# One stage in place of two: output projection, norm and FFN of a layer

## The reference, cut to what matters

```
x = x + gate1 * (mixed @ w_out)                 # output projection, 1024 x 1024
h = rmsnorm(x, norm2_g) * (1 + scale2) + shift2 # mean of squares over the 1024 features of a token
a, b = split(h @ w_ffn_in)                      # 1024 x 5632
x = x + gate2 * ((silu(a) * b) @ w_ffn_out)     # 2816 x 1024
```

## Time and profile before

| | |
|---|---|
| median of 3 runs | 3119.05 us (3117.54 to 3120.02) |
| the profiled execution | 3119.82 us, of which the span is 3118.0 us |
| TensorE busy | 2794.0 us, 90% of the span |
| VectorE busy | 1394.4 us, 45% |
| ScalarE busy | 832.1 us, 27% |
| GpSimd busy | 727.8 us, 23% |
| mean granted TensorE clock | 0.947 |

### The profile page before, as it was taken

The page is one execution under the profiler, slowest core; times in us unless marked ns, Lnnn a source line. Parts: engine busy times, 40 slices in busy tenths (PEclk is TensorE's granted clock), DMA queues, the critical chain, the costliest instruction groups (busy, mean ns, idle before and its releaser), DMA issues. The chain is left out here.

```text
span 3118.0 us, 41354 instructions
## 1 busy us (share of the span) xinstructions
PE 2794.0 (90%) x16562; PEld 2658.8 (85%) x16562; DVE 1394.4 (45%) x2937; ACT 832.1 (27%) x1235; POOL 727.8 (23%) x279
## 2 busy tenths in 40 slices
PE   6994886969999999999589996889699999999995
PEld 4994775969999999999479995549699999999994
DVE  6996885672322222223445554543623222222235
ACT  4112665052111111111442222541521111111114
POOL 1551123142112211111231112332421122111110
PEclk9996998979999999999799997999899999999997
DMA  5433100412111111110223335304021111111101
GB/s 229 144 120 78 21 8 33 173 58 81 41 40 40 40 50 44 40 40 0 114 77 142 142 123 203 105 19 176 34 81 41 40 40 41 51 43 40 40 0 61
DMA packets 59395, 225.92 MB, mean 72 GB/s; under 512 B 7136, under 2 KB 20128, under 8 KB 49696
## 3 DMA queue, kind: packets, MB, share of 16 engines
q1 hardware_dynamic: 57712, 224.07, 20.3%
q10 hardware_dynamic: 1584, 0.51, 0.1%
HBM read 190.47 MB, written 29.88 MB: 71 GB/s over the span
## 5 line engine op out<-in xcount | busy, mean ns | idle before, releaser
L420 PE MATMUL ps<-hh,wi_hi 128*128 128x384 f32 x2112 | 710.3, 336 | 8.9 <-POOL hl L335 4.6
L421 PE MATMUL ps<-hl,wi_hi 128*128 128x384 f32 x2112 | 709.5, 336 | 0.0
L422 PE MATMUL ps<-hh,wi_lo 128*128 128x384 f32 x2112 | 709.4, 336 | 0.0
L802 DVE TENSOR_TENSOR hid<-ps,hid 128x384 f32<-128x384 f32 x132 | 73.4, 558 | 1048.6 <-ACT hid L712 1019.3
L420 PEld LDWEIGHTS ps<-hh,wi_hi 128*128 128x128 f32 x2112 | 399.0, 189 | 12.8 <-POOL hl L335 5.6
L421 PEld LDWEIGHTS ps<-hl,wi_hi 128*128 128x128 f32 x2112 | 399.4, 189 | 0.0
L422 PEld LDWEIGHTS ps<-hh,wi_lo 128*128 128x128 f32 x2112 | 399.2, 189 | 0.0
L712 ACT ACTIVATE hid<-ps 128x384 f32<-128x384 f32 x132 | 65.0, 493 | 1178.1 <-PE ps L422 1178.1
L792 DVE SCALAR_TENSOR_TENSOR x<-ps,mod,x 128x128 f32<-128x128 f32 (+1 forms) x704 | 327.3, 513 | 77.7 <-PE ps L422 72.9
L735 POOL TENSOR_TENSOR wi_lo<-raw_in,wi_hi 128x2048 fp32r<-128x2048 f32 x44 | 202.5, 4604 | 681.4 <-ACT wi_hi L703 681.4
L421 PE MATMUL ps<-hid_lo,wo_hi 128*128 128x384 f32 x1056 | 353.0, 334 | 0.0
(11 more groups left out here) (231 smaller groups left out, 3983.2 us busy)
## 6 DMA issues: line engine op xcount, KB each, us to landing
raw_in<-in_w_ffn_in_dram SPq DMA_DIRECT2D x44, 1024.0 KB, 4.7
wmt<-in_w_mod_t_dram SPq DMA_DIRECT2D x80, 512.0 KB, 3.6
raw_out<-in_w_ffn_out_dram SPq DMA_DIRECT2D x22, 1024.0 KB, 4.7
gla_spill<-turn SPq DMA_DIRECT2D x24, 576.0 KB, 2.8
raw<-in_w_in_odd_dram SPq DMA_DIRECT2D x24, 512.0 KB, 3.9
wm<-in_w_mod_dram SPq DMA_DIRECT2D x16, 512.0 KB, 11.3
raw<-in_w_in_even_dram SPq DMA_DIRECT2D x16, 512.0 KB, 4.4
x<-in_x_dram SPq DMA_DIRECT2D x4, 1152.0 KB, 9.6
```

What stands on the lines that cost most here:

```text
L420: pe.matmul(acc, w_hi, in_hi, start=first, stop=False)
L421: pe.matmul(acc, w_hi, in_lo, start=False, stop=False)
L422: return pe.matmul(acc, w_lo, in_hi, start=False, stop=last)
L802: dve.tensor_tensor(hid[:, t], ps[:, 2 * t + 1, 0:CW], hid[:, t], ALU.mult).then_inc(hid_done, 1)
```

## The change

`projection` and `ffn` of a layer become one stage, `trunk`, with one instruction order written out by hand for each engine:

- x is loaded in four transfers of two tiles each (`stream`) straight into x and is updated in place. `x_old` is gone. SyncE issues only the first of the four ahead of weight tiles 2 and 3.
- `whi` and `wlo` have three buffers each. Tiles 0 to 5 are multiplied as before. The last pair is multiplied third by third: (6,0), (7,0), (6,1), (7,1), (6,2), (7,2).
- Squares are taken on ScalarE as each third of each tile is finished, and summed on GpSimd (`Seam.square`, `Seam.total`), into the space of `raw_out`.
- The norm is done for each third on its own: mean by TensorE, Ln and Exp by ScalarE, `scale` by VectorE, shift and high part together by ScalarE, low part by VectorE. It is placed among the last tiles of the projection and the first blocks of pass 0.
- In pass 0 the six hidden blocks run one after the other, and the contractions of thirds 0 and 1 follow.
- The first FFN weights are loaded, cast and split during tiles 4 to 6.
- In `ModulationBeside`, one instruction over 1024 columns takes the place of four over 256 with their final sum. This holds for all four stages that use it. In `trunk` each third of a tile has one modulation tile beside it, from third 0 of tile 0 on, until the 16 (layer 0) or 8 (layer 1) are used up.

The diff, cut to its core (`Attended` and `Ready`, which did nothing, go; semaphores and buffer offsets are left out):

```diff
-                for g in range(self.SEGS):
-                    seg = slice(g * w, (g + 1) * w)
-                    last = dve.scalar_tensor_tensor(out=self.unused[:, 0, seg], in0=self.wmt[t % 2][:, seg], scalar=1.0,
-                                                    in1=self.silu_row[:, v, seg], op0=ALU.mult, op1=ALU.mult,
-                                                    accum_out=self.part[:, t, v, g:g + 1])
...
+                if 2 * n + v:
+                    dve.wait_ge(self.wmt_used, 2 * n + v)
+                dve.scalar_tensor_tensor(out=self.unused, in0=self.wmt[n % 2][:], scalar=1.0, in1=self.silu_row[:, v],
+                                         op0=ALU.mult, op1=ALU.mult, accum_out=self.acc[:, n % 4, v:v + 1]).then_inc(self.wmt_used, 1)
...
+        def total(self, pool, ft, c):
+            e, a = self.place[ft, c]
+            if a is None:
+                return
+            pool.wait_ge(self.squared, e + 1)
+            if a:
+                pool.wait_ge(self.summed, a)
+            pool.tensor_tensor(self.stat[:, c], self.stat[:, c], self.sq[a % 2][:], ALU.add).then_inc(self.summed, 1)
+        def mean(self, pe, c, bank):
+            pe.wait_ge(self.summed, self.adds[c])
+            pe.matmul(bank, ones[:], self.stat[:, c], start=True, stop=True).then_inc(self.averaged, 1)
+        def root(self, act, c, bank):
+            act.wait_ge(self.averaged, c + 1)
+            act.activation(self.stat[:, c], bank, ACT.Ln, bias=eps[:], scale=1.0 / D).then_inc(self.logged, 1)
+            act.wait_ge(self.logged, c + 1)
+            act.activation(self.stat[:, c], self.stat[:, c], ACT.Exp, scale=-0.5).then_inc(self.rooted, 1)
+        def scale(self, dve, c, kk):
+            if kk == 0:
+                dve.wait_ge(self.rooted, c + 1)
+            for cols, v in pieces[c]:
+                loc = slice(cols.start - c * CW, cols.stop - c * CW)
+                last = dve.scalar_tensor_tensor(out=hl_f32[:, kk, cols], in0=x[:, kk, cols], scalar=amod[:, self.n, kk, v:v + 1],
+                                                in1=self.stat[:, c, loc], op0=ALU.mult, op1=ALU.mult)
+            last.then_inc(self.scaled, 1)
+        def high_part(self, act, c, kk):
+            act.wait_ge(self.scaled, KT * c + kk + 1)
+            for cols, v in pieces[c]:
+                last = act.activation(hh[:, kk, cols], hl_f32[:, kk, cols], ACT.Identity,
+                                      bias=mod[:, self.layer, self.shift * KT + kk, v:v + 1])
+            last.then_inc(self.high, 1)
+        def low_part(self, dve, c, kk):
+            dve.wait_ge(self.high, KT * c + kk + 1)
+            for cols, v in pieces[c]:
+                last = dve.scalar_tensor_tensor(out=hl[:, kk, cols], in0=hl_f32[:, kk, cols],
+                                                scalar=mod[:, self.layer, self.shift * KT + kk, v:v + 1],
+                                                in1=hh[:, kk, cols].bitcast(F32), op0=ALU.add, op1=ALU.subtract)
+            last.then_inc(self.low, 1)
+        def through(self, dve, c, a, b):
+            for kk in range(a, b):
+                if kk < KT:
+                    self.scale(dve, c, kk)
+                if kk >= 2:
+                    self.low_part(dve, c, kk - 2)
...
+    def trunk(layer, w_dram, residual, in_hi, in_lo, first_mod, groups, scales=()):
...
+            tile_off = [o, o + 2 * WB, W0 + 12 * WB]
...
+            bank_at = lambda m, c: ps[:, NC * (m % 2) + c, 0:CW]
+            mean_bank = [ps[:, b, 0:CW] for b in (0, 3, 5)]
...
+                def stream(g):
+                    sp.dma_start(x[:, 2 * g:2 * g + 2], residual[:, 2 * g:2 * g + 2]).then_inc(x_in[g], 16)
...
+                weights(0)
+                weights(1)
+                stream(0)
+                mods.load_row(sp)
+                mods.load(sp, 0)
+                mods.load(sp, 1)
+                weights(2)
+                weights(3)
+                for g in range(1, KT // 2):
+                    stream(g)
+                for n in range(2, MODS):
+                    mods.load(sp, n)
+                    if n % 3 == 1 and n // 3 + 3 < KT:
+                        weights(n // 3 + 3)
+                for m in range(min((MODS - 1 - 1) // 3 + 3, KT - 1) + 1, KT):
+                    weights(m)
+                load_in(0, 0)
+                load_in(0, 1)
+                sp.wait_ge(norm.scaled, KT * NC)
+                load_out(0)
...
+                cast(0)
+                cast(1)
+                mods.silu(act)
+                cast(2)
+                for m in range(LAST - 1):
+                    for c in range(NC):
+                        square(m, c)
                 cast_in(0, 0)
                 cast_in(0, 1)
-                norm.act_late(act)
-                body(0, first=True)
+                for c in range(NC):
+                    square(LAST - 1, c)
+                square(LAST, 0)
+                square(LAST + 1, 0)
+                square(LAST, 1)
+                norm.root(act, 0, mean_bank[0])
+                for kk in range(KT):
+                    norm.high_part(act, 0, kk)
+                    if kk == KT // 2:
+                        square(LAST + 1, 1)
+                square(LAST, 2)
+                square(LAST + 1, 2)
+                norm.root(act, 1, mean_bank[1])
+                for kk in range(KT):
+                    norm.high_part(act, 1, kk)
+                silu(0, 0, 0)
+                norm.root(act, 2, mean_bank[2])
+                for kk in range(KT):
+                    norm.high_part(act, 2, kk)
+                    if kk == KT // 2:
+                        silu(0, 0, 1)
+                hidden_high(0, 0)
+                cast_out(0)
+                silu(0, 1, 0)
...
+                pool.wait_ge(w_low, KT)
+                split_in(0, 0)
+                for c in range(NC):
+                    norm.total(pool, LAST - 1, c)
+                pool.wait_ge(multiplied, NC * LAST)
+                split_in(0, 1)
+                for c in range(NC):
+                    norm.total(pool, LAST, c)
+                    norm.total(pool, LAST + 1, c)
+                split_out(0)
...
+                tile(LAST, 0)
+                tile(LAST + 1, 0)
+                tile(LAST, 1)
+                pe.wait_ge(taken, place[LAST, 0] + 1)
+                norm.mean(pe, 0, mean_bank[0])
+                tile(LAST + 1, 1)
+                tile(LAST, 2)
+                tile(LAST + 1, 2)
+                pe.wait_ge(taken, place[LAST + 1, 0] + 1)
+                norm.mean(pe, 1, mean_bank[1])
+                pe.wait_ge(win_low, 2)
+                pe.wait_ge(norm.logged, 1)
+                pe.wait_ge(taken, place[LAST, 1] + 1)
+                hidden(0, 0, 0, first=True)
+                pe.wait_ge(taken, place[LAST + 1, 2] + 1)
+                norm.mean(pe, 2, mean_bank[2])
+                pe.wait_ge(norm.logged, 2)
+                pe.wait_ge(taken, place[LAST, 2] + 1)
+                hidden(0, 0, 1)
+                for c in (1, 2):
+                    for t in range(2):
+                        pe.wait_ge(hid_done, 2 * c + t - 1)
+                        hidden(0, c, t, first=t == 0)
+                contract(0, 0)
+                contract(0, 1)
...
+                        last = dve.scalar_tensor_tensor(out=x[:, m, cols], in0=bank_at(m, c)[:, loc],
+                                                        scalar=mod[:, layer, GATE1 * KT + m, v:v + 1], in1=x[:, m, cols],
+                                                        op0=ALU.mult, op1=ALU.add)
+                    last.then_inc(taken, 1)
...
+                for m in range(LAST):
+                    for c in range(NC):
+                        evict(m, c)
+                        if place[m, c] < MODS:
+                            mods.multiply(dve, place[m, c])
+                mods.finish(dve)
+                evict(LAST, 0)
+                evict(LAST + 1, 0)
+                evict(LAST, 1)
+                norm.through(dve, 0, 0, 5)
+                evict(LAST + 1, 1)
+                norm.through(dve, 0, 5, KT + 2)
+                evict(LAST, 2)
+                evict(LAST + 1, 2)
+                norm.through(dve, 1, 0, KT + 2)
+                gated(0, 0, 0)
+                norm.through(dve, 2, 0, 6)
+                gated(0, 0, 1)
+                norm.through(dve, 2, 6, KT + 2)
+                hidden_low(0, 0)
+                for c in (1, 2):
+                    gated(0, c, 0)
+                    gated(0, c, 1)
+                    hidden_low(0, c)
+                add(0, 0)
+                add(0, 1)
...
-    projection(inp["w_out_even"], KT, W0, residual=(inp["x"], 0, GATE1),
-               prepare=partial(Attended), mods=(6 * KT, 4, (2,)))
-    ffn(0, norm=dict(n=1, layer=0, shift=SHIFT2))
+    trunk(0, inp["w_out_even"], inp["x"], lambda kk, cols: (o_hi[kk] if kk < HEADS else p_hi[kk - HEADS])[:, cols],
```

(41 more changed lines are left out.)

508 lines of the change are left out of this document (157 added, 351 removed).

## The result

The changed kernel takes 3042.85 us (median of 4 runs, 3040.77 to 3044.89) where the kernel before takes 3118.3 (median of 4, 3117.54 to 3120.02): a ratio of 0.9763, interval 0.9751 to 0.9775. The forecast was 3041, by the case called A. The medians differ by 75.5 us, 2.4 less than the 77.8 of the forecast. The profiled execution took 3040.77 us, 79.05 less than the one before. This is where they went; a stretch's loss is its length less 0.1733 us for each product started in it, as in the prediction.

The account below looks back on a forecast made before the run. TensorE, busy 90% of the span, bounds the kernel, so only its lost stretches count: 4.1 + 8.7 + (38.7 - 5.3) + (36.9 - 5.3) = 77.8 us off 3119.8, 3042.0, median 3041; range 3032 to 3060.

Parts of the forecast that it names:

- the case called A: The forecast itself for the whole kernel, 3041 us, own range 3037 to 3047; chance 0.58.
- if TensorE waits before the first hidden block: Sign of a wrong prediction, in the seam: TensorE's first hidden block was to start at 26.6 us with no wait.
- Modulation at the end of `opening`: One 1024-column instruction, 1.28 us, lets VectorE finish sooner at the end of `opening`: 4.1 us gained, bounds 2.5 and 4.1.
- Elsewhere VectorE works beside a dense TensorE, and the saving is worth nothing: Outside the end of `opening`, the shorter modulation was to gain 0 us.
- rival E: Slower than before: VectorE becomes the projection's pace, its evictions and modulation holding up TensorE; 3143 us, chance 0.03.
- A third costs VectorE 3.5 us against 4.16, so it catches up: Projection thirds with a modulation tile: eviction 0.6 us plus multiplication 2.85, within TensorE's 4.16 us.
- Start of `trunk(0)`: Layer 0's first projection: weight tiles 2 and 3 issued earlier end the stall at tile 2; 8.7 us gained, bounds 0 and 8.8.
- The seam: Projection to FFN in each layer: 5.3 us lost, 2.4 for means and 2.9 of waits, where 38.7 and 36.9 were.
- waits at (1,1) and (2,0): In the seam, TensorE waits for gating ahead of these FFN blocks, 1.5 and 1.4 us.
- The table loads: ScalarE's norm roots: Ln and Exp each load a table, 1.28 us, by the rows; one shared set would give 3038 us.
- rival D: Means and waits in the seams all but vanish, 1.4 us to a seam; 3033 us, chance 0.07.
- Rival B: The seam's chain stretches as GpSimd stops VectorE's scalings and low parts, 8 us more a seam; 3057 us, chance 0.20.

Follow-up runs that it names:

- e2: The changed kernel with modulation's four instructions of 256 columns and their sum put back; 3064.89 us, ratio 0.9825.
- e3: The changed kernel with the old SyncE order, all of x and four modulation tiles ahead of weight tiles 2 and 3; 3051.42 us.
- e6: The changed kernel with GpSimd's sums of (6,0) and (7,0) ahead of `split_in(0,1)` and the sum of (7,1) on VectorE; 3035.76 us.
- e11: e6 with the root's Exp replaced by Identity with bias 1, so the norm is wrong, to price table loads; 3031.68 us.
- e4: The changed kernel with the sums of (6,0) and (7,0) ahead of `split_in(0,1)` on GpSimd; 3044.31 us, ratio 0.9757.
- e9: e6 with VectorE's sum of (7,1) one operation pair earlier, ahead of scaling 6; 3041.72 us, ratio 0.9755.
- e10: e9 with the last two evictions among third 0's VectorE operations, their squares earlier on ScalarE, sums of (6,2) and (7,2) on VectorE; 3035.43 us.

## Why the prediction was right, point by point

The time was right, the stall and the chain of thirds were right, and the waits of the seams were not. The prediction's own sign of being wrong, "if TensorE waits before the first hidden block", came about in both layers: mean 1 stands directly ahead of that block and waits 1.25 and 4.00 us.

- **Modulation at the end of `opening`: right.** 1.23 us for 1024 columns (1.28 forecast), first transfer at 251.21 (250.9), 3.7 us of 4.1.
- **"Elsewhere VectorE works beside a dense TensorE, and the saving is worth nothing": wrong.** With the quarters put back the changed kernel loses 13.9 us in layer 0. The step read the cost of quarters (3.0 us a tile) and the new sums on GpSimd each by itself. Together they make a third 4.45 us on VectorE, over TensorE's 4.16. The same edit that was priced at 4 us is also what keeps rival E away.
- **"A third costs VectorE 3.5 us against 4.16, so it catches up": near, and too kind.** It is 3.62, since the sum stops the second multiplication for 0.6 us each time (1.86 in place of 1.22), and with the split and the closing additions 12.5 us for a tile of 12.5. VectorE didn't catch up: it stayed 4.3 us behind until tile 5, and the FFN weights that wait for it on SyncE were late with it, and so, behind their split, was mean 0 of layer 0, while layer 1, with 8 modulation tiles, has no wait there. The argument against E, 5.3 us of GpSimd on 10.5 of VectorE, is 15.8 us for a tile of 12.5: it rules out the loss of the whole gain, not a lag of 3 us a tile, and `e2` has that lag.
- **Start of `trunk(0)`: right** in size and cause (`e3`). VectorE stood for modulation tile 2, as forecast, for 5.22 us, until 20.1 us after the first product (24 reckoned).
- **The seam: the chain was right, the waits were not.** 8.2 and 7.7 us where 5.3 was forecast. The term that failed is "Mean 0 runs 12.5 to 13.3, no wait" and "Total (7,1) is done at 23.5": the first left out that GpSimd's queue has `split_in(0,1)` ahead of the sums, the second let a sum of 1 us be 1 us beside VectorE's dense run (it was 5.49). The 2.9 us of waits at (1,1) and (2,0) are real, `e6` measures 2.1 of them, but stood behind these. The means cost 0.65 each, not 0.8.
- **The table loads: right to go by the rows.** The rule of one set, put inside rival D, would have needed roots without a load between Ln and Exp, and every root has one. Where it held it would be worth more than the 2.6 us reckoned, since the root of third 1 would need no load at all (`e11`).
- **Rival B** named the port and looked for its price on VectorE's operations. These kept their step of 0.53 and 0.66 us. GpSimd paid it. The Trainium skill (SBUF — State Buffer, Who interferes with whom) has whoever comes second wait out a whole instruction; VectorE's 1.86 us beside a sum and its 4.41 beside a split agree with that; the sum's wait for a dozen instructions goes beyond it.
- **Attention's 5.2 us** were no part of the sum. Executions of kernels that leave it alone cover 283.3 to 288.8 in that stretch; the profiled execution of before was the longest, that of after near the shortest. Between the profiled executions this scatter (5.2) and the rest (1.6) outweighed the seams' shortfall (5.2) and that of `opening` (0.4), so the sum was met within 1.2 us, by chance; between the medians the gain is 2.4 us short of it.

## What to carry to other kernels

When work is moved under a busy engine, add up each helper engine's cost per round with the new neighbours in place, and compare it with the round: 4.45 us against 4.16 and a stop for a split cost 14 us, 3.62 and the same stop came out level. Follow the small operations on the path through their own queue and past whoever shares their port; put a 1 us sum on the engine whose dense run would hold it up. And of several waits in a row, only the chain that ends last is worth shortening: `e4` and `e9` each moved a wait and gained nothing, `e10` and `e11` shortened the chain and gained. `e10` beats both kernels, 3035.43 us, its interval just clear of the changed kernel's on the same chip; of those 7 us the seams explain 4.7.

## What the runs showed of the hardware

- A GpSimd sum of 1.01 us that starts within a run of VectorE instructions with two SBUF inputs lasts until the run ends (5.49 us, in `e4` too), while VectorE steps on unhindered. The other way round, one VectorE instruction is stopped once by a sum, 1.86 us in place of 1.22, and one of 8 columns took 4.41 us in place of 0.17 beside a split of 4.72.
- A wait of TensorE costs more than itself: over a mean without a wait, 4.00 us ahead of mean 1 in layer 1 lost 5.7, 2.83 ahead of mean 0 in layer 0 lost 4.7, and 0.98 in `e6` only 1.2. Right after the first two the granted clock is 0.50, the lower of its two levels (1.2 GHz); after the 1.25 us ahead of mean 1 in layer 0 it is 1.00.
- Attention, which no edit touched, with the start of the projection behind it took 283.3 to 288.8 us over 14 profiled executions. What sets it wasn't tried.
